# Earlier weight loads during the merge, a ninth weight buffer, and small matmuls in TensorE's waits

## The reference

```
x = x + (g_a * (y_a @ w_br_a) + g_b * (y_b @ w_br_b)) @ w_out
h = rms_norm(x, norm_ffn)
logits = h @ w_router + b_router;  top 4 of 32, softmax over the four
expert e:  clamped_swiglu(h @ w_up[e] + b_up[e]) @ w_down[e] + b_down[e]
x = x + sum over the four experts of weight * expert output;  y = rms_norm(x, norm_final)
```

## Time and profile before

| what | us |
|---|---|
| median of three runs | 1440.2 |
| lowest and highest | 1438.92, 1441.64 |
| the profiled execution, its device time | 1438.51 |
| its span in the profile | 1436.6 |
| TensorE busy in it | 1336.5 |

### The profile page before, as it was taken

One profiled execution on the slowest core, in us unless ns is written; L12 is line 12 of the kernel. 1 busy time (PEld: TensorE's weight loads), 2 busy tenths in 40 slices (PEclk: granted clock), 3 DMA queues, 4 the chain that ended last, 5 costly groups with the idle time before them and its releaser, 6 DMA issues.

```text
span 1436.6 us, 20588 instructions
## 1 busy us (share of the span) xinstructions
PE 1336.5 (93%) x8365; PEld 663.5 (46%) x8366; DVE 495.3 (34%) x1055; ACT 189.9 (13%) x407; POOL 101.9 (7%) x150
## 2 busy tenths in 40 slices
PE   6998879899999989999999999999999999999995
PEld 6887867687778523332333233333333333233231
DVE  3455556424551413232323223224222322233224
ACT  3221113323410300000000000000000000000001
POOL 1002032330000000000000000000000000000000
PEclk9999989899999999999999999999999999999998
DMA  6333248184488899999999999999999999999993
GB/s 213 118 93 91 64 108 269 41 276 146 150 215 341 337 431 429 431 430 431 431 431 431 431 431 432 430 430 431 431 429 433 430 432 431 431 432 430 431 431 133
DMA packets 94195, 479.94 MB, mean 334 GB/s; under 512 B 12740, under 2 KB 61110, under 8 KB 69176
## 3 DMA queue, kind: packets, MB, share of 16 engines
q1 hardware_dynamic: 85832, 452.00, 77.7%
q0 software_dynamic: 7600, 25.45, 4.9%
q10 hardware_dynamic: 704, 1.63, 0.3%
HBM read 478.60 MB, written 8.56 MB: 339 GB/s over the span
## 4 chain that ended last, share of the span: by engine, by line
DMA 33%; PE 32%; DVE 1%; issue 1%; ACT 0%; SPq 0%; DVEq 0%; ACTq 0%
DMA ring<-in_w_up 33%; PE bank L2430 18%; PE bank L2451 7%; PE bank L2405 2%; PE bank L2444 1%; PE bank L2417 1%; DVE x L2268 1%; PE bank L2387 1%; PE bank L2036 0%; PE bank L2022 0%; PE bank L2393 0%; DVE ring L2356 0%; PE bank L2043 0%; DVE x L2365 0%; PE bank L2014 0%
## 5 line engine op out<-in xcount | busy, mean ns | idle before, releaser
L2430 PE MATMUL bank<-ring,ex_work 128*64 128x512 f32 x2048 | 464.9, 603 | 24.4 <-DMA ring<-in_w_up 24.4
L2430 PEld LDWEIGHTS bank<-ring,ex_work 128*64 128x64 f32 x2048 | 140.9, 138 | 333.9 <-issue 274.3
L2451 PE MATMUL bank<-ring,ex_work 128*64 128x512 f32 x1024 | 233.6, 610 | 0.0
L2279 DVE TENSOR_SCALAR ex_work<-bank 128x512 f32<-128x512 f32 x32 | 22.1, 691 | 401.6 <-PE bank L2430 401.6
L2268 DVE TENSOR_TENSOR x<-bank,x 128x512 f32<-128x512 f32 (+1 forms) x192 | 117.2, 670 | 101.5 <-PE bank L2405 101.5
L2451 PEld LDWEIGHTS bank<-ring,ex_work 128*64 128x64 f32 x1024 | 72.2, 140 | 159.1 <-issue 159.1
L2405 PE MATMUL bank<-ex_work,ex_back 64*128 64x512 f32 x384 | 91.1, 606 | 1.5 <-ACT ex_work L2199 1.5
L558 PE MATMUL bank<-hT,w_group 128*128 128x264 f32 (+1 forms) x400 | 90.1, 387 | 0.0
L558 PEld LDWEIGHTS bank<-hT,w_group 128*128 128x128 f32 (+1 forms) x400 | 74.3, 186 | 14.7 <-issue 0.7
L2161 POOL DMA_INDIRECT ex_work<-scratch_h,ex_si x31 | 31.7, 1022 | 603.1 <-PE bank L2387 602.3
L2193 ACT ACTIVATE ex_work<-ex_work 128x512 f32<-128x512 f32 x32 | 20.1, 629 | 382.0 <-DVE ex_work L2279 382.0
(11 more groups left out here) (485 smaller groups left out, 1180.8 us busy)
## 6 DMA issues: line engine op xcount, KB each, us to landing
ring<-in_w_up SPq DMA_DIRECT2D x128, 2048.0 KB, 24.1
ring<-in_w_down SPq DMA_DIRECT2D x64, 2048.0 KB, 26.8
w_group<-in_w_in SPq DMA_DIRECT2D x12, 1024.0 KB, 5.3
w_cmp<-in_w_in SPq DMA_DIRECT2D x8, 1024.0 KB, 8.7
sel_rows<-in_w_out SPq DMA_DIRECT2D x8, 512.0 KB, 7.3
out_win_s<-in_state_win_kv POOLq DMA_DIRECT2D x1, 4088.0 KB, 28.9
x<-in_x_prompt SPq DMA_DIRECT2D x4, 512.0 KB, 4.9
win_rows<-in_state_win_kv SPq DMA_DIRECT2D x4, 512.0 KB, 4.9
```

Source lines behind the costliest of these rows:

```text
L2430: mm = mmul(banks[n // 2][lo:lo + SLOTS, :], B["xT"][:, k % 4, SLOTS * (k // 4):SLOTS * (k // 4) + SLOTS], slot_of(k)[:, 512 * n:512 * n + ...
L2451: mm = mmul(banks[4][SLOTS * n:SLOTS * n + SLOTS, :], B["hT"][:, k % 4, SLOTS * (k // 4):SLOTS * (k // 4) + SLOTS], slot_of(8 + 4 * half + ...
```

## The change

Five things are changed.

1. In the merge, w_out goes to pairs 2 and 3 (rows of 4 KB) and no longer to pieces of 512 bytes in `sel_rows`.
2. SP loads the first two quarters of expert 0's w_up, waits for `ab` to reach 8, loads all four halves of w_down of experts 0 and 1, waits for `od` to reach 8 (w_out is then used), and loads the last two quarters of expert 0.
3. The tables of the routing that are needed later (`one_hot`, `rt_rank_k`, `extra_base`, and with them `first_rows`) move to the spare area. Where the routing's other temporaries lie, a ninth buffer is put. VectorE signals `routes_done` after its last routing step, SP waits for it and loads the first quarter of expert 1 there. Pair 0, which expert 1 does not use, takes the first quarter of expert 2 directly after the loads of expert 1. From expert 2 on the ring is the old one.
4. Seven calls of `filled` put 17 matmuls of the identity with 256 columns into TensorE's program; nothing reads their results.
5. PE waits count accordingly.

The diff, cut to its core:

```
+        ninth = at("ring_ninth", [P, 2, 2 * FF], TEMPS)
...
-        def upper_weights(sp, e):
-            for q in range(4):
+        def upper_weights(sp, e, parts):
+            for q in parts:
                 sp.dma_start(pairs[q][:], a["w_up"][0][e, 256 * q:256 * q + 256, :].rearrange("(p c) n -> p c n", c=2)).then_inc(ring_in[2 * q], 16)
+
+        def lower_weights(sp, e):
+            for j in range(2):
+                slot = 8 + 4 * e + 2 * j
+                sp.dma_start(pairs[slot // 2][:], a["w_down"][0][e, 512 * j:512 * j + 512, :].rearrange("(p b c) n -> p b (c n)", b=2, c=2)).then_inc(ring_in[slot], 16)
...
+        def filled(bank, n):
+            for _ in range(n):
+                nc.tensor.matmul(bank[:, 0:2 * P], ident, masks[:, 0:2 * P], start=True, stop=True)
...
                     mm.then_inc(so, 1)
+                    filled(banks[6], 4)
...
+                        if b == 1:
+                            filled(banks[3], 2)
...
                     layer1(NR - 2)
                     layer1(NR - 1)
+                    filled(banks[2], 4)
...
                     mm.then_inc(vc, 1)
+                    filled(banks[2], 2)
...
+                def wo(c):
+                    return pairs[2 + c // 4][:, c % 4 // 2, D * (c % 2):D * (c % 2) + D]
...
                     for c in range(KD):
-                        sp.dma_start(sel[:, c, :, :, P:256], a["w_out"][0][P * c:P * c + P, :].rearrange("p (a b n) -> p a b n", a=2, b=4)).then_inc(wo_in, 16)
+                        sp.dma_start(wo(c), a["w_out"][0][P * c:P * c + P, :]).then_inc(wo_in, 16)
...
                     sp.wait_ge(outs.sem, 16 * 9)
-                    upper_weights(sp, 0)
+                    upper_weights(sp, 0, (0, 1))
+                    sp.wait_ge(ab, KD)
+                    for e in range(2):
+                        lower_weights(sp, e)
+                    sp.wait_ge(od, KD)
+                    upper_weights(sp, 0, (2, 3))
...
-                            mmul(banks[m % 2][:, 0:T], sel[:, c, m // 4, m % 4, P:256], mix[:, c, :], start=(c == 0), stop=False)
+                            mmul(banks[m % 2][:, 0:T], wo(c)[:, P * m:P * m + P], mix[:, c, :], start=(c == 0), stop=False)
...
                     mm.then_inc(partd, 1)
+                    filled(banks[7], 1)
...
+            own = at("first_rows", [P, 3, SLOTS], SPARE + 7680)
+            oh = at("one_hot", [P, 3, TOPK, NEXP], SPARE + 8448)
+            rki, base = at("rt_rank_k", [P, 3, TOPK], SPARE + 9984), at("extra_base", [P, NEXP], SPARE + 10048)
...
-                down(0)
-                down(1)
+                sp.wait_ge(S["routes_done"], 1)
+                sp.dma_start(ninth[:], a["w_up"][0][1, 0:256, :].rearrange("(p c) n -> p c n", c=2)).then_inc(S["ninth_in"], 16)
...
-                step(nc.vector.tensor_copy(over[:], ov[:]))
+                nc.vector.tensor_copy(over[:], ov[:]).then_inc(S["routes_done"], 1)
+                dve.wait_ge(S["routes_done"], 1)
...
                     mm.then_inc(signal, 1)
+                filled(banks[6], 2)
...
                 mm.then_inc(rkd, 1)
+                filled(banks[6], 2)
...
-                    def up(e, wait):
-                        for q in range(4):
-                            if wait and q < 3:
+                    def up(e, wait, parts=range(4), first_free=False):
+                        for q in parts:
+                            if first_free and q == 0:
+                                sp.wait_ge(S["up_used"], 1)
+                            elif wait and q < 3:
...
-                    up(1, True)
-                    with sp.Fori(1, NEXP // 2) as pair:
+                    up(1, True, (1, 2, 3))
+                    up(2, True, first_free=True)
+                    down(2, 0, True)
+                    up(3, True)
+                    down(3, 1, True)
+                    with sp.Fori(2, NEXP // 2) as pair:
...
+                            if first_pair is not None and k == 0:
+                                pe.wait_ge(first_pair, 16)
+                            elif k == 0:
+                                pe.wait_ge(ring_in[k], 16 * e)
+                            elif k % 2 == 0:
                                 pe.wait_ge(ring_in[k], 16 * (e + 1))
...
-                                          slot_of(k)[:, 512 * n:512 * n + 512], start=False, stop=(k == KD - 1))
+                                          (ninth[:, k, :] if e_ninth and k < 2 else slot_of(k))[:, 512 * n:512 * n + 512], start=False, stop=(k == KD - 1))
...
-                    up(0, False, 0)
+                    up(0, False, 0, False, ring_in[0])
                     turn_x(1)
-                    up(1, True, 0)
+                    up(1, True, 0, False, S["ninth_in"], True)
```

More of the change, by code:

```diff
@@ L1812, in expert_buffers @@
             for n in ("up_used", "down_used", "x_in", "x_turned", "xT_ready", "up_done", "g_ready", "sig_ready", "h_ready",
[L1813 removed]
+                      "h_turned", "hT_ready", "down_done", "y_ready", "tw_read", "back_ready", "comb", "added", "u_read", "idx", "pick_up", "pick_down", "bias_in", "rows_stored", "table_read", "routes_done", "ninth_in"):
                 S[n] = sem("ex_" + n)
@@ L1825, in route @@
             tsum = sb(st, "top_sum", [P, 3])
-            oh = sb(st, "one_hot", [P, 3, TOPK, NEXP])
             asg = sb(st, "assigned", [P, 3, NEXP])
             rank = sb(st, "rank", [P, 3, NEXP])
-            cnt, extra, base = sb(st, "counts", [P, NEXP]), sb(st, "extra", [P, NEXP]), sb(st, "extra_base", [P, NEXP])
+            cnt, extra = sb(st, "counts", [P, NEXP]), sb(st, "extra", [P, NEXP])
             tmp = sb(st, "route_tmp", [P, NEXP])
-            rki, part, slot, ocol, first = (sb(st, "rt_" + n, [P, 3, TOPK]) for n in ("rank_k", "part", "slot", "ocol", "first"))
+            part, slot, ocol, first = (sb(st, "rt_" + n, [P, 3, TOPK]) for n in ("part", "slot", "ocol", "first"))
             cell = at("cells", [P, 3, TOPK, 2, NEXP], SPARE + 3072)
@@ L1834, in route @@
             ohr, xeq = at("one_hot_times", [P, 3, TOPK, NEXP], SPARE + 6144), at("extra_hit", [P, 3, TOPK, MORE], SPARE + 7680)
-            own = at("first_rows", [P, 3, SLOTS], SPARE + 9216)
+            own = at("first_rows", [P, 3, SLOTS], SPARE + 7680)
+            oh = at("one_hot", [P, 3, TOPK, NEXP], SPARE + 8448)
+            rki, base = at("rt_rank_k", [P, 3, TOPK], SPARE + 9984), at("extra_base", [P, NEXP], SPARE + 10048)
             hit = xT[:].rearrange("p a b -> p (a b)")[:, 0:3 * TOPK * P].rearrange("p (a b c) -> p a b c", a=3, b=TOPK)
@@ L1850, in sp_routes @@
             def sp_routes(sp):
-                def down(e):
-                    for j in range(2):
-                        slot = 8 + 4 * e + 2 * j
-                        sp.dma_start(pairs[slot // 2][:], a["w_down"][0][e, 512 * j:512 * j + 512, :].rearrange("(p b c) n -> p b (c n)", b=2, c=2)).then_inc(ring_in[slot], 16)
                 for i in range(2):
@@ L2407, in comb, with up @@
                                 mm.then_inc(S["comb"], 1)
-                    def up(e, wait, back, late=False):
+                    def up(e, wait, back, late=False, first_pair=None, e_ninth=False):
                         if late:
```

2 lines of the change are left out of this document (removed).

## The result

The changed kernel takes **1445.81 us** (median of 6 runs, 1442.85 to 1448.16), the kernel before 1439.56 us beside it (6 runs, 1435.8 to 1441.94). The ratio is 1.0049, with a 95% interval of 1.0034 to 1.0064. It is slower by 6 to 7 us, about 0.5%. The forecast was 1441.4, the range ended at 1445.5. The profiled execution of the changed kernel took 1445.24 us, its span is 1443.2, against 1436.6 before.

The account below looks back on a forecast made before the run. The weight-load stream was taken as the bound. +1.5 us (later fourth quarter) and -0.3 (fills) gave +1.2 on the 1436.6 span, 1437.8; with 1.9 around it 1439.7, and 1.7 to the median, 1441.4 us; range 1434.5 to 1445.5.

Parts of the forecast that it names:

- What bounds the kernel: Expert stage: weight loads at 431 GB/s take 29.2 us per expert, TensorE 27.4, so the load stream's start decides.
- The gain on offer: Restart of the load stream after routing: 6.2 us outstanding before, less 1.4 us to first bytes, a 4.8 us lead.
- What delays the routing's end: VectorE's wait for six bias loads queued behind eight pair loads: biases there near 497, routing ends 7.5 us later.
- the lagging half: Half of the DMA engines carry the window-state copy, 19.4 us each, and so run late with the pair loads.
- the biases need 1.8 us at the full rate: Transfer time of the bias loads behind the last quarters, with 1.4 us more added to the semaphore.
- the second rival: Biases are later still: their own transfer takes 5.3 us, not 1.8, everything shifts 3.5 us, 1444.9 us; chance 0.24.
- The chain behind the biases: VectorE's remaining routing steps after the bias wait, 6.7 us together, ending the routing at 503.7.
- From the ninth's issue to the fourth quarter's landing: Ninth pair issued at 503.7, fourth quarter of expert 1 lands at 526.4, 0.6 us later than before; +1.5 us taken.
- TensorE's late start as cover: Expert 0 starting 7 us later costs nothing, as TensorE gains 1.8 us per expert on the loads over 28 more.
- The third rival: The cover fails: TensorE idles from 491, begins expert 0 at the lower clock, costing some 1.8 us; 1443.2; chance 0.07.
- The fills: 17 filling matmuls in TensorE's waits raise its clock: -0.3 us taken from a range of -1.7 to +0.6.
- The loads win: First rival: biases come by 487, routing ends at 496.1, the 4.8 us lead remains; 1434.8 us; chance 0.17.

Follow-up runs that it names:

- c4: Changed kernel with window copy on sixteen engines, biases ahead of the two last upper quarters, trimmed biases, and no ninth pair; ratio 0.9937 to the kernel before.
- d2: Kernel before, without the early loads, with the window copy on sixteen engines and the trimmed biases; ratio 0.9971 to the kernel before.
- d1: Changed kernel with the same bias bytes written to 128 partitions instead of 32, in shorter packets; ratio 0.9994 to the kernel before.
- b1: Changed kernel with VectorE's wait for the biases and its two copies moved behind the last routing step; 1445.34 us.
- a3: Changed kernel with the window-state copy cut into 16 x 8 pieces so that all sixteen DMA engines share it; 1435.7 us.
- b2: Changed kernel without the ninth pair, expert 1's first quarter going to pair 0 as before; 1444.99 us.
- a4: Changed kernel without its 17 filling matmuls; 1446.7 us.
- a2: Changed kernel with the two last upper quarters issued behind the bias loads in SP's queue instead of ahead; 1437.27 us.
- c1: Changed kernel with window copy on sixteen engines, biases ahead of the two last upper quarters, and trimmed biases; ratio 0.9936 to the kernel before.

## Why the prediction was wrong

**What bounds the kernel** was right: the rate from the sixteenth slice on is the same. But TensorE's first wait for a quarter came later than foretold. It ends at 715.2, in the eighth expert after expert 0 and not some five experts after it. In the kernel before, TensorE waits briefly during expert 1 and then again from 649 on, in the sixth after expert 0.

**The gain on offer** was right in size: 4.8 us foretold, 5.0 by the spans and expert 0's start, 4.9 (1.6 to 8.2) between c4 and d2. The agreement to 0.2 us is partly luck. By expert 0's start the two profiles of c4 and d2 are 3.8 us apart (937.7 and 941.5), and c4 and the kernel before 6.3.

**What delays the routing's end** was right in mechanism and too small, and this is the step that failed. By landings: the last of the six pairs was to land at 482.8 (481.6 and 1.2 us to the semaphore) and landed at 482.4. So the lagging half, the copy's 19.4 us and the start of the stream together came out right. The two last quarters were to land at 494.5 (482.8 and 9.7 for their bytes and 2.0 for the stored rows) and landed at 498.3, **3.8 us late**. The biases were to follow by 2.0 us and followed by 3.6, **1.6 us late**. Both belong to one mis-sized term, "the biases need 1.8 us at the full rate": on the early half they held up the packets from 482 to 488, the two quarters on the late half among them (with the biases spread, in d1, 3.5 of these 3.8 us are gone), and on the late half, from 496 to 500, they moved at 203 and then 114 GB/s, with stored rows between them. Together 5.4 us, and 501.9 instead of 496.5, which the prediction rounded to 497. The price stood in the second rival: 5.3 us for their transfer, read from the trace of the kernel before. Its time, 1444.9, is 0.9 us from the result. The prediction gave it 0.24, because "fewer loads run beside them now". In fact the last two quarters still ran beside them on the late half, and were slowed as well.

Both parts could have been read from the kernel before, where the prediction misread two rows. Its check put the slow half's end at 476.4. But the last quarter, issued at 437.7, took 42.6 us and so landed at 480.4, 2.8 us later than 476.4 and 1.2: it was held up there already, in the stretch of 171 and 203 GB/s shown above. And the 4.2 to 5.1 us to landing are those of the four bias loads alone. The two loads of the picks, for which VectorE also waits, took 4.7 and 6.9:

```profile
477.06 0.42 SPq L1860 DMA_DIRECT2D ex_pick<-in_c_pick  x1
DMA to landing us min/median/max: 6.9/6.9/6.9
```

So all six were there at 483.9, not 481.7, and 3.6 us after the last quarter, the very distance of the changed kernel. With 2.8 more for the quarters and 3.6 instead of 2.0 behind them the sum gives 500.9, 1.0 us from the landing, and a time of 1445.3.

**The chain behind the biases** was right: 6.7 us foretold, 6.6 measured (501.9 to 508.5).

**From the ninth's issue to the fourth quarter's landing.** Foretold were 22.7 us (503.7 to 526.4), measured 23.7 (508.5 to 532.2). So the quarter landed 6.4 us later than before, and the span is 6.6 us longer. The rule that the landing of this quarter carries over to the end held. With the biases' true landing the same sum would have given a result of about 1446.

**TensorE's late start as cover** was the wrong picture, though it did no harm to the sum. The prediction said that the ninth's issue restarts the stream and expert 0's start hides behind it. b1 shows the opposite: the ninth can leave 11.6 us earlier for nothing, because every load behind it waits for expert 0. In the changed kernel both hang on the biases by chains of like length, so either view gave the same number, by luck. The third rival, TensorE's lower clock, seems to have a part in the result: with the clock at 0.50 from 494 on, expert 0 takes 15.28 us where it took 13.95, 1.3 us more where the rival said 1.8. Over the kernels with eight pairs ahead, the distance from expert 0's start to the end grows with that time, from 937.7 us (c4, 13.95) to 941.0 (a3, 16.68). No run changed the clock alone.

**The ninth pair** gains nothing: right (b2, c4). **The fills**: -0.3 us foretold in a range of -1.7 to +0.6; a4's median lies 0.9 us higher, which is less than can be told.

**The rivals.** "The loads win" (1434.8) did not happen in the changed kernel, but a2 and a3 (1437.3, 1435.7) come near it once the biases are early, and c1 goes past it.

The range ended 0.3 us below the result. Its upper end was put where the second rival stood with hardly anything beyond, although the bound of 501 for the biases' landing alone would have given 1445.4. The measured landing was 0.9 us past that bound, because the bound took the slow transfer alone, and not what it does to the quarters in front.

## What to carry to other kernels

When loads are moved ahead, look at the small loads that now stand behind them: the last of those to land, not the big ones, sets when the work starts. Price a small load by what it took in the trace, to the landing of the last of those that are waited for, not by its bytes, above all where it goes to a few partitions; if it was slow before, take the slow price, and charge its neighbours too. And capacity in a ring helps only as long as its own transfer time is; past that, the first consumer's start decides, so first bring that start forward.

## What the runs showed of the hardware

- Loads to 32 partitions at a time slowed the loads beside them: 181 GB/s with the engines 0.98 busy, and 368 with the same bytes spread over 128 partitions in shorter packets. The busy share does not show it, the rate does.
- A DRAM-to-DRAM copy in 8 rows took 29.3 us and left the stream at half rate behind it (205 GB/s, engines 0.48 busy); in 16 x 8 pieces it took 21.1 us, and the stream ran at 442 GB/s.
- Trimming a third of those bytes (0.26 MB) brought the landing 2.8 us forward, while at 431 GB/s they are 0.6 us.
- Executions of one kernel family reach the same point of the program up to 7 us apart (first quarter issued at 426.06 to 432.55) with nothing changed ahead of it, so single profiles are compared from a mark and not from zero.
